# A two-layer decoder trunk on one core: the HGRN2 gate and key on ScalarE, level products on half columns, and a reordered prologue

## What is computed

```
h = RMSNorm(x) * (1 + scale) + shift        # shift, scale, gate = silu(c) W_mod + b_mod
P = h W_in                                  # HGRN2 q f i g | MLA c_q c_kv k_rope g | retention q k v g | 3 merge logits
y_b = mixer_b(...) * silu(gate_b)           # b in HGRN2, MLA, retention
m = sum_b sigmoid(merge_b) * (y_b W_p,b)
x = x + gate * (m W_out)                    # and a last RMSNorm after layer 2
```

```
f = lb + (1 - lb) * sigmoid(z)      k = (1 - lb) * sigmoid(-z)      g = log f
S_t = diag(f_t) S_{t-1} + k_t i_t^T          o_t = S_t^T q_t
```

## Time and profile before

| | |
|---|---|
| median of 3 runs | 1389.4 us (1388.32 to 1389.75) |
| profiled execution | 1386.04 us, of which the span of the trace is 1384.2 |
| PE busy | 1306.4 us, 94% |
| DVE, ACT, POOL busy | 724.0, 639.5, 590.7 us |
| mean granted clock of PE | 0.986 of full |
| DMA | 131.84 MB, mean 95 GB/s |
| layer 0's first product of `first_batch` | at 32.7 us |

### The profile page before, as it was taken

The page is one execution under the profiler, slowest core; times in us unless marked ns, Lnnn a source line. Parts: engine busy times, 40 slices in busy tenths (PEclk is TensorE's granted clock), DMA queues, the critical chain, the costliest instruction groups (busy, mean ns, idle before and its releaser), DMA issues.

```text
span 1384.2 us, 16588 instructions
## 1 busy us (share of the span) xinstructions
PE 1306.4 (94%) x5920; PEld 1036.3 (75%) x5920; DVE 724.0 (52%) x1163; ACT 639.5 (46%) x987; POOL 590.7 (43%) x751
## 2 busy tenths in 40 slices
PE   3999889999999999999979988999999999999996
PEld 2877777787777777788858777778777777778884
DVE  6778786534654434353356777662345431433333
ACT  3365545544554343444335555554355434435431
POOL 3254334654323445455526334445532253454551
PEclk9999999999999999999989999999999999999998
DMA  9322111443222323242212211123312222222221
GB/s 363 121 77 63 60 62 63 142 136 102 77 78 101 126 84 116 98 134 95 94 68 92 77 61 62 65 72 122 107 54 69 77 92 84 91 84 93 98 92 61
DMA packets 40786, 131.84 MB, mean 95 GB/s; under 512 B 5248, under 2 KB 5376, under 8 KB 39424
## 3 DMA queue, kind: packets, MB, share of 16 engines
q1 hardware_dynamic: 30336, 111.57, 23.5%
q10 hardware_dynamic: 10368, 19.21, 4.6%
HBM read 128.13 MB, written 2.10 MB: 94 GB/s over the span
## 4 chain that ended last, share of the span: by engine, by line
PE 80%; DVE 13%; ACT 4%; issue 2%; DMA 1%; POOL 0%; DVEq 0%; ACTq 0%
PE ps_st L760 20%; PE ps_st L762 20%; PE ps_st L761 20%; PE ps_o L782 5%; PE ps_s L811 2%; PE ps_s L856 2%; PE ps_s L880 1%; PE ps_w L865 1%; DVE hg_at L1434 1%; DVE hg_e L1367 1%; PE ps_misc L777 1%; DVE cq_raw L1604 1%; DVE hg_e L1366 1%; PE ps_w L726 1%; PE ps_misc L768 1%
## 5 line engine op out<-in xcount | busy, mean ns | idle before, releaser
L643 POOL TENSOR_TENSOR w_lo<-raw,w_hi 128x256 fp32r<-128x256 f32 x736 | 579.7, 822 | 752.6 <-ACT w_hi L934 752.6
L760 PE MATMUL ps_st<-h_hi,w_hi 128*128 128x512 f32 x984 | 400.3, 407 | 1.0 <-DVE merged L1303 1.0
L762 PE MATMUL ps_st<-h_hi,w_lo 128*128 128x512 f32 x984 | 383.9, 390 | 0.0
L761 PE MATMUL ps_st<-h_lo,w_hi 128*128 128x512 f32 x984 | 383.3, 390 | 0.0
L760 PEld LDWEIGHTS ps_st<-h_hi,w_hi 128*128 128x128 f32 x984 | 184.8, 188 | 45.8 <-issue 7.4
L761 PEld LDWEIGHTS ps_st<-h_lo,w_hi 128*128 128x128 f32 x984 | 185.0, 188 | 42.0 <-issue 6.2
L762 PEld LDWEIGHTS ps_st<-h_hi,w_lo 128*128 128x128 f32 x984 | 184.7, 188 | 39.6
L934 ACT ACTIVATE w_hi<-raw 128x1024 fp32r<-128x1024 f32 x184 | 193.2, 1051 | 26.6 <-PE ps_st L762 23.5
L956 ACT ACTIVATE gate_t<-gate_x 128x512 f32<-128x512 f32 x80 | 50.4, 630 | 230.5 <-DVE gate_x L1252 230.3
L1252 DVE TENSOR_SCALAR gate_x<-ps_st 128x512 f32<-128x512 f32 x79 | 54.4, 689 | 192.0 <-PE ps_st L762 191.8
L958 ACT ACTIVATE gate_t<-gate_t,cs 128x512 f32<-128x512 f32 x80 | 57.9, 724 | 2.6
(11 more groups left out here) (280 smaller groups left out, 2014.5 us busy)
## 6 DMA issues: line engine op xcount, KB each, us to landing
raw<-w_stream SPq DMA_DIRECT2D x184, 512.0 KB, 3.4
mod_w<-w_mod ACTq DMA_DIRECT2D x64, 256.0 KB, 2.7
pro_w<-w_mod_first SPq DMA_DIRECT2D x8, 1024.0 KB, 14.0
x<-x_t SPq DMA_DIRECT2D x4, 512.0 KB, 7.5
ret_decay<-decay ACTq DMA_DIRECT2D x2, 1024.0 KB, 6.3
out_t<-o_t SPq DMA_DIRECT2D x8, 256.0 KB, 2.1
raw_extra<-w_stream SPq DMA_DIRECT2D x2, 512.0 KB, 20.0
cs<-cst SPq DMA_DIRECT2D x1, 836.0 KB, 7.8
```

What stands on the lines that cost most here:

```text
L643: ins = nc.gpsimd.tensor_tensor(lo[:, r], whole[:, r], hi[:, r].bitcast(F32), ALU.subtract)
L760: nc.tensor.matmul(dst[0:m, :], wh, hi, start=(k == 0), stop=False)
L761: nc.tensor.matmul(dst[0:m, :], wh, lo, start=False, stop=False)
L762: last = nc.tensor.matmul(dst[0:m, :], wl, hi, start=False, stop=(k == nk - 1))
```

## The change

1. **Gate and key.** ACT goes on in place behind sigmoid(z): an Ln with scale and bias gives log f in hz_c. sigmoid(-z) stays in hz_a, and ACT makes the key from it with a scaled Copy. DVE's two tensor_scalars go; `hz 2` is the scan.
2. **Order.** `hg_out` of head h - 2 moves from group q to group i, `hz 1` behind `ex 5`. `hg_v` writes bank "misc".
3. **Half columns.** Levels 0 to 4: the product is made for the second halves of each block alone, 64 columns per chunk, and copied with copy_predicated from a half bank. hg_at's diagonal blocks are zeroed once per layer.
4. **Prologue.** Positions and parameters load first, on SP's queue; x on ACT's. One function table for Exp and Ln is loaded first. DVE makes the angles ahead of the lower bounds. x * rstd is made by POOL into four slots, ACT scales, shifts and rounds it, DVE subtracts. Sin comes behind tile 4 instead of tile 2. Item g starts with tile 4 instead of 5.

```diff
-BATCH_START = (0, 1, 2, 3, 5)
+BATCH_START = (0, 1, 2, 3, 4)
...
-                [("hz", h, 1), ("sel", b, 2), ("sel", b, 3), ("xb", b, 4), ("hz", h, 2), ("ex", b, 5), ("mm", b, 4),
-                 ("hg_out", h - 2)],
-                [("sel", b, 4), ("xb", b, 5), ("ex", b, 6), ("hz", h, 3), ("ex", h, 0), ("ex", h, 1), ("mm", b, 5)],
+                [("sel", b, 2), ("sel", b, 3), ("xb", b, 4), ("ex", b, 5), ("hz", h, 1), ("mm", b, 4)],
+                [("sel", b, 4), ("xb", b, 5), ("ex", b, 6), ("hz", h, 2), ("ex", h, 0), ("ex", h, 1), ("mm", b, 5),
+                 ("hg_out", h - 2)],
...
         elif kind == "hg_v":
-            use("o", s)
+            use("misc", s)
...
+            sp.dma_start(pos_i[:], positions[0:1, :].to_broadcast([P, SEQ])).then_inc(pos_in, 16)
+            sp.dma_start(cur[:], params_cur[0]).then_inc(cur_in, 16)
+            sp.dma_start(nxt[:], params_nxt[DEPTH]).then_inc(par_in, 16)
...
+                def scale_x(j):
+                    if j == 0:
+                        pool.wait_ge(rstd_ready, 1)
+                    if j >= 4:
+                        pool.wait_ge(norm_hi, j - 3)
+                    nc.gpsimd.tensor_tensor(x_rstd[:, j % 4, :], x[:, j, :], rstd[:], ALU.mult).then_inc(x_scaled, 1)
                 for i, it in enumerate(ITEMS):
+                    if layer == 0 and i < len(BATCH):
+                        for j in ((0, 1), (2,), (3,), (4,), (5,))[i]:
+                            scale_x(j)
+                    elif layer == 0 and i == len(BATCH):
+                        scale_x(6)
+                        scale_x(7)
...
+                            if n < 5:
+                                late = right[:, r].rearrange("p (b s m) -> p b s m", s=2, m=LEVELS[n])[:, :, 1, :]
+                                last = nc.tensor.matmul(dst[:, k * P // 2:(k + 1) * P // 2], left[:, r], late, start=True, stop=True)
...
-            act.dma_start(pos_i[:], positions[0:1, :].to_broadcast([P, SEQ])).then_inc(pos_in, 16)
-            act.dma_start(nxt[:], params_nxt[DEPTH]).then_inc(par_in, 16)
-            act.dma_start(cur[:], params_cur[0]).then_inc(cur_in, 16)
+            for j in range(0, DT, 2):
+                act.dma_start(x[:, j:j + 2, :], x_t[:, j:j + 2, :]).then_inc(x_in[j // 2], 16)
+            act.preload_act_table_set(TABLE_SET)
...
                         A(hz_c[:], hz_b[:], ACT.Exp, scale=-1.0).then_inc(act_link, 1)
+                        act.wait_ge(act_link, e.made(act_link))
+                        A(hz_c[:], hz_c[:], ACT.Ln, scale=one_lb[:, j:j + 1], bias=lb[:, j:j + 1]).then_inc(log_f, 1)
...
+                            act.wait_ge(x_scaled, j + 1)
+                            act.wait_ge(scale_ready, j + 1)
+                            if j >= 2:
+                                act.wait_ge(h_ready, e.at(h_ready, j - 1))
+                            A((t1, t2)[j % 2][:], x_rstd[:, j % 4, :], ACT.Identity, scale=scale_g[:, j:j + 1],
+                              bias=shift[:, j:j + 1]).then_inc(norm_t, 1)
+                            act.wait_ge(norm_t, e.at(norm_t, j + 1))
+                            A(h_hi[:, j, :], (t1, t2)[j % 2][:], ACT.Copy).then_inc(norm_hi, 1)
...
-                        A(hz_b[:], hz_a[:], ACT.Exp, scale=-1.0).then_inc(hz_s, 1)
-                    elif kind == "hz" and s[2] == 2:
-                        act.wait_ge(hz_f, e.at(hz_f, s[1] + 1))
-                        A(hz_a[:], hz_a[:], ACT.Ln).then_inc(hz_l, 1)
+                        A(hz_a[:], hz_a[:], ACT.Exp, scale=-1.0).then_inc(act_link, 1)
                         act.wait_ge(act_link, e.made(act_link))
+                        A(hg_k[:, h % 2, :], hz_a[:], ACT.Copy, scale=one_lb[:, h:h + 1]).then_inc(k_built, 1)
...
+                    V.tensor_copy(carry[:], one)
+                    if n < 5:
+                        m = LEVELS[n]
+                        b = P // (2 * m)
+                        dst = diagonal(hg_at[h % 2]).rearrange("p c (b s m) -> p c b s m", s=2, m=m)[:, :, :, 1, :]
+                        mask = mask.rearrange("p (b s m) -> p b s m", s=2, m=m)[:, :, 1, :]
+                        src = ps[:, 0:SEQ // 2].rearrange("p (c b m) -> p c b m", b=b, m=m)
+                        ins = V.copy_predicated(dst, mask[:, None, :, :].to_broadcast([P, CH, b, m]), src)
```

More of the change, by code:

```diff
@@ L810, in _ @@
                             r = slice(k * P, (k + 1) * P)
-                            last = nc.tensor.matmul(dst[:, r], left[:, r], right[:, r], start=True, stop=True)
+                            if n < 5:
+                                late = right[:, r].rearrange("p (b s m) -> p b s m", s=2, m=LEVELS[n])[:, :, 1, :]
+                                last = nc.tensor.matmul(dst[:, k * P // 2:(k + 1) * P // 2], left[:, r], late, start=True, stop=True)
+                            else:
+                                last = nc.tensor.matmul(dst[:, r], left[:, r], right[:, r], start=True, stop=True)
                         done(last, ("lv", h, n))
@@ L1325, in hz @@
                     if n == 1:
+                        if h == 0:
+                            for t in hg_at:
+                                V.memset(diagonal(t), 0.0)
                         dve.wait_ge(hz_ln, e.at(hz_ln, h + 1))
@@ L1385, in level_operands @@
                     dve.wait_ge(e_ready, e.at(e_ready, 7 * h + n + 1))
+                    if e.new(k_built, h + 1):
+                        dve.wait_ge(k_built, e.at(k_built, h + 1))
                     if 2 <= n < 5:
@@ L1422, in level_select @@
                     ps = bank[e.bank_of(("lv", h, n))]
[L1423 to L1424 removed]
+                    mask = c(("m64", "m32", "m16", "m8", "m4", "mbase")[n]).bitcast(U32)
                     if n == 0:
```

60 lines of the change are left out of this document (24 added, 36 removed).

## The result

The changed kernel takes 1377.99 us (median of 7 runs, 1376.54 to 1383.76) against 1389.75 for the kernel before in the same runs (7 runs, 1388.32 to 1393.28). The profiled execution took 1380.03 us, its span is 1378.2.

The account below looks back on a forecast made before the run. PE's stream and its stalls were taken to bound the kernel. Terms 28.2 - 6 + 0 + 1.5 + 3.5 = 27.2 us less took the profiled 1386.04 us to 1358.8, with 3.4 for the median 1362.2 us; range 1346 to 1381.

Parts of the forecast that it names:

- What bounds the kernel: Whole run: PE, busy 1306.4 of 1384.2 us; only less work in its stream or less standing still shortens it.
- hg_kd, 28.2 us: PE's eight waits for hg_kd (21.8 us) and the slow clock behind four (6.4 us) go: 28.2 us gained.
- The wait that takes its place, 6 us: At hg_v, PE waits for bank misc, freed by ACT's Ln, in 4 places: 6 us lost.
- I take 1.5 us each: Length taken for each of the 4 new waits of PE for misc at hg_v, without slow clock.
- The sum's own end for this step, 19 us: Worst case for the 4 waits for misc: 4 x (3 + 1.7) = 19 us, with the slow clock.
- given back: Rival, chance 0.18: misc wait 3.5 to 4 us with slow clock, or DVE late; 16 us less gain, 1378.
- Half columns, 0 us: Level products, 320 records on PE: 64 columns take the same 107 to 110 ns as 128, so 0 us.
- The products pay too: Rival, chance 0.07: columns set the pace of the level products and PE gains 17 us: 1345.
- slower: gapped columns: Rival, chance 0.05: gapped operands of the level products read at double time, 34 us lost: 1396.
- hg_x at head 0, a gain of 1.5 us: PE's wait for hg_x, mostly at head 0, shrinks as the scan comes a step earlier: 1.5 us gained.
- Prologue, 3.5 us: Start of the kernel: earlier angles and modulation gain 4.4 us, PE waits about 1 us at item 5; 3.5 left.
- a wait at L768 of over 3 us with the clock at 0.50 behind it: Sign of being wrong: PE's wait for ACT's rstd at hg_v exceeds 3 us and brings the halved clock.

Follow-up runs that it names:

- e4: The changed kernel with ACT's Ln and Exp of the output of head h-2 put ahead of exponentials ex 2 and ex 3: 1356.31 us.
- e8: The kernel before with only hg_out one item later and hg_v into bank misc; gate and key stay on DVE: 1374.88 us.
- e7: e4 with level products and selections on whole columns again: 1358.81 us.
- e2: The kernel before with parts 1 to 3 of the change, prologue left old: 1372.51 us.
- e6: e4 with the prologue of the kernel before: 1357.63 us.
- e10: e8 with e4's edit, gate and key on DVE, whole columns, old prologue: 1361.82 us.
- e9: e5 with the level products' operands xb 0 and xb 1 of layer 0's head 0 made one item earlier: median 1360.38 us.
- e5: e4 with exponentials ex 0 and ex 1 of layer 0's head 0 one item earlier: 1356.13 us.
- e13: e9 with the prologue of the kernel before: ratio 0.9753 to the kernel before.
- e15: e13 with the new prologue's loads, table load and angles, but x times rstd on DVE, without POOL's products: 1352.61 us.
- e3: The kernel before with the prologue part (part 4) alone: 1388.24 us.
- e11: The kernel before, unchanged, profiled again in one execution: 1387.15 us.
- e18: e12 unchanged, as control on the same chip as e16: ratio 0.975 to the kernel before.
- e16: e12 with x times rstd made by DVE in place of POOL: ratio 0.9752 to the kernel before.
- e12: e9 unchanged, run again: ratio 0.9763 to the kernel before.

## Why the prediction was wrong in size

- **What bounds the kernel** was right: PE's stream, and the stalls in it.
- **hg_kd, 28.2 us**: right, and a little too small. In e4, where nothing takes their place, heads 1 to 3 and the tails of both layers are 31.4 us shorter than before (the rows of the table from head 1 on, layer 1's "heads 0 and 1" among them, with a wait for hg_x of 1.1 us in it). What the prediction had for head 1, that DVE's savings cover its 1.8 us, is what e8 and e4 show; the rest is the order's alone.
- **The wait that takes its place, 6 us**, is the step that failed. It cost 31.4 us less the 14.1 us that after gains in the same rows: 17.3 us. Of these 8.4 are the waits, which leaves 8.9 for the lower clock behind them (17.0 us at half rate, which is 8.5). "I take 1.5 us each" went wrong twice. The eight half-tiles behind hg_kd were taken at the 3.3 us of the kernel before; the first two ran beside POOL and took 0.96 us in place of 0.41 (which the prediction names, but puts into the end of the range only), so misc came free 5.0 us behind hg_kd in place of 4.0 and each wait was 2.1 us. And the clock was costed at nothing, since no wait of up to 1.8 us in the kernel before had brought the lower level; here 2.1 us brought it in three of four places. The sum's own end for this step, 19 us, was close in total, not in its parts (12 + 6.8 against 8.4 + 8.9). The rival "given back" gave the measured time, 1378 us, but partly by luck: it has waits of 3.5 to 4 us that cost 16 us more than the sum, where the waits were 2.1 us and cost 11.3 more, and the rest came from head 0 and the prologue.
- **Half columns, 0 us**: right. 1.71 us for sixteen in either kernel, and e7 finds nothing elsewhere. The rule of the Trainium skill that was weighed (TensorE: Matmul & The Clock Gate, "LDWEIGHTS") gives about 107 ns for 128 columns of weights; the trace agrees with it, 1.71 us / 16 = 107 ns per record of 64 columns. "The products pay too" and "slower: gapped columns" fall with it.
- **hg_x at head 0, a gain of 1.5 us**: wrong in sign for layer 0. Its head 0 takes 33.48 us in place of 30.75. ACT's added Ln and Copy sit in the chain that hg_q, and with it hg_x, waits for, the square sum of cq 1 stands in front of hg_x, and the wait, 1.1 us at most before, grew to 3.0 us and had the lower clock behind it for 6.8 us. The runs narrow it down to part 1: e2 and e6 with the old prologue and e7 with whole columns have the wait (2.9 to 3.0 us), e8 and e10 with gate and key on DVE don't; the queue inside part 1 is read off the timelines. "ACT gets one operation more per head (0.6 us)" counted the operation but not what queues behind it. With e9's order head 0 takes 30.4 us, with 3.4 us at the lower clock left in it.
- **Prologue, 3.5 us**: wrong. Its timeline in after:

```profile
7.80 0.43 DVE L1517 CAST pos_f<-pos_i 128x512 f32<-128x512 int32 x1 [2.00 <-DMA pos_i<-positions]
...
20.14 0.49 DVE L1535 TENSOR_SCALAR ps_o<-pro_w,cond 128x256 f32<-128x256 f32 x1
...
38.24 0.85 PE L744 MATMUL ps_w<-cond,pro_w 128*128 128x1 f32 x4
...
78.51 0.47 PE L778 MATMUL ps_st<-h_hi,w_hi 128*128 128x512 f32 x1 [1.22 <-POOL w_lo L661]
```

  The positions landed at 7.8 us, not 6.3, and the first term came at 20.14, 1.3 us earlier, not 3.8. Tile 3's column stands at 38.24 against 42.38, 4.1 us earlier where 4.4 were forecast; that agreement is partly luck, since the first column gained 1.3 us (24.65 to 23.38) in place of 2.9 and the later rounds more than they were given. The wait of 1 us at item 5 came as foreseen. What was not foreseen came between: the held low part, 5.6 us of PE's time, and a stretch at the lower clock behind it. In e4, e5 and e9, whose change of pace was early and whose low part was not held, the new prologue is worth 2.4 to 2.6 us at item 5 (71.61 to 71.86 against 74.22). Without POOL's products the new loads, table and angles are worth 2.4 us (e13 to e15, 73.82 to 71.44 at item 5; 1.8 us by the medians of their ratios, less than their intervals tell apart). "Which POOL makes beside it" was costed at nothing: the products join POOL's work to one stretch that lasts until 49 us, and DVE stands still for it in 5 of 11 profiled executions. The profile of after has lost 4.3 us there, e3 gains nothing in the median.
- **Sum against the profile of before**: 31.4 - 17.3 - 2.7 (head 0) - 4.3 (prologue) = 7.1 us; 1.0 us is lost at the rest of layer 0 and the start of layer 1, 0.1 in the last stretch, which makes the 5.9 us seen within rounding. Against the 27.2 of the forecast that is 11.3 for the wait, 7.8 for the prologue and 4.2 for head 0, less 3.2 that hg_kd gave on top. The direction and the range held, since they took in "given back".
- What the prediction named as a sign of being wrong, "a wait at L768 of over 3 us with the clock at 0.50 behind it", was set too high: 2.1 us did it in three of four places.

Open: why PE's change of pace in the prologue comes at 39 to 42 us in some executions and beyond 46 in others. It comes late in 7 of the 11 profiles with POOL's products and in 2 of the 9 without (e10, e11), costs 2.6 us at item 5 from before to e11 and 4.6 from e9 to e18, and no run here isolates it. Why the low part is held in some executions and not in others, with POOL's work the same, and why only that of tile 3, is open too; so is why a wait of one length has the lower clock behind it in one place and not in another.

## What to carry to other kernels

When a step is moved to take it off one engine's path, look on every other engine for what it now stands behind: here one Ln on an engine that was idle for 5 us, placed behind a pair that waits, cost 14 to 17 us, and moving it in front gave them back. Cost a new wait of PE with the clock drop that may follow, also when it is no longer than waits that went free elsewhere: here waits of 1.8 us had the drop behind them in some places and not in others. When the end of the range is that close, take it rather than the middle. Work that is given to an idle POOL is not free for DVE: e15 and e16 keep the products off POOL and have no held low part (gaps in POOL's stretch were not tried). Judge such a step over several executions, since one profile may show either case.

## What the runs showed that I had not expected

- DVE's instruction with two inputs in SBUF (128x512) took 6.1 to 7.6 us in place of 0.7, until POOL's unbroken 25 us of two-input instructions had ended (about 0.55 us after POOL's end in all five); both forms of it did (7.64, 6.83). POOL stretches of 6.5 us (e15) and 13.4 us (e16) held none. Beside POOL's low parts a 128x256 product took 0.95 us in place of 0.41 at the places shown.
- The length of a wait of PE doesn't tell whether the lower clock follows. Over the heads of all twenty profiles, 3.4 or 6.8 us of it came with 8 of 18 waits of 1.76 to 1.84 us (e10's above, and the wait for POOL's w_lo in e9, e12, e13 and e15 to e18), with 7 of 12 of 2.07 to 2.23 us, 2 of 4 of 2.4 to 2.5 us, all 8 of 2.9 to 3.0 us and 11 of 12 of 3.7 to 3.8 us.
- In the prologue records of 512 columns stand 0.43 us apart, then 0.23 (e18), while the granted clock of the profile shows 1.00 for both; eight other profiles show 0.50 for the slow part. There the distance of records tells the pace more surely than the column of the clock.
